# Four units of a banded attention transposed by VectorE and DMAs, with their products four steps later

## What is computed

```python
scores = jnp.einsum('bnqgrd,bnkgd->bngrqk', qb, kb) * (HEAD_DIM ** -0.5)
bias = -slopes[:, :, None, None] * dist[None, None]
scores = jnp.where(mask[None, :, None, None], scores + bias[None, None], -jnp.inf)
m = jnp.maximum(jnp.max(scores, axis=-1, keepdims=True), sink_l)
p = jnp.exp(scores - m)
denom = jnp.sum(p, axis=-1, keepdims=True) + jnp.exp(sink_l - m)
probs = (p / denom).astype(v.dtype)
out = jnp.einsum('bngrqk,bnkgd->bnqgrd', probs, vb)
```

## Time and profile before

| | us |
|---|---|
| median of 3 runs | 612.68 |
| lowest, highest | 609.06, 613.05 |
| the profiled execution | 608.62 |
| its span | 606.8 |
| granted clock of TensorE over the span | 0.999 of full |
| busy PE, DVE, ACT, POOL | 596.5, 447.3, 356.3, 293.6 |

### The profile page before, as it was taken

The page is one execution under the profiler, slowest core; times in us unless marked ns, Lnnn a source line. Parts: engine busy times, 40 slices in busy tenths (PEclk is TensorE's granted clock), DMA queues, the critical chain, the costliest instruction groups (busy, mean ns, idle before and its releaser), DMA issues.

```text
span 606.8 us, 9197 instructions
## 1 busy us (share of the span) xinstructions
PE 596.5 (98%) x3076; PEld 482.6 (80%) x3076; DVE 447.3 (74%) x802; ACT 356.3 (59%) x762; POOL 293.6 (48%) x273
## 2 busy tenths in 40 slices
PE   8999999999999999999999999999999999999996
PEld 7888887888888888888887777777767777888885
DVE  5786653334434439889999788998988988799884
ACT  6645133113333238777886678888788788534563
POOL 4610704415756432536547545876776776510601
PEclk9999999999999999999999999999999999999999
DMA  7598458574776620101005967868767745598042
GB/s 252 188 285 237 118 163 267 198 274 138 249 271 224 209 69 1 36 1 36 2 26 129 256 146 177 204 165 194 186 155 198 196 136 182 179 383 323 1 171 108
DMA packets 72431, 102.11 MB, mean 168 GB/s; under 512 B 10232, under 2 KB 43008, under 8 KB 72384
## 3 DMA queue, kind: packets, MB, share of 16 engines
q1 hardware_dynamic: 72224, 101.25, 55.6%
q10 hardware_dynamic: 160, 0.27, 0.1%
HBM read 60.17 MB, written 31.62 MB: 151 GB/s over the span
## 4 chain that ended last, share of the span: by engine, by line
PE 88%; DVE 4%; ACT 3%; DMA 2%; issue 1%; POOL 1%; SPq 0%; ACTq 0%
PE ps L1821 18%; PE ps L1823 17%; PE ps L1822 17%; PE ps L2115 8%; PE ps L2093 7%; PE ps L2023 5%; PE ps L2028 4%; PE ps L1993 3%; PE ps L2043 2%; PE ps L2003 2%; PE ps L1980 2%; PE ps L1979 2%; PE ps L2004 2%; ACT p_b L1221 1%; DVE pT_lo L1671 1%; DVE stat L1646 1%
## 5 line engine op out<-in xcount | busy, mean ns | idle before, releaser
L1671 DVE TENSOR_TENSOR pT_lo<-ps,pT_hi 128x512 fp32r<-128x512 f32 x102 | 68.8, 687 | 23.5 <-ACT pT_hi L1234 23.3
L1821 PE MATMUL ps<-hT_hi,w_hi 128*128 128x512 f32 x208 | 84.0, 404 | 0.0
L1221 ACT ACTIVATE p_b<-ps,stat 128x1024 f32<-128x1024 f32 x64 | 71.4, 1116 | 19.3 <-DVE stat L1646 19.0
L1823 PE MATMUL ps<-hT_hi,w_lo 128*128 128x512 f32 x208 | 81.4, 391 | 0.0
L1822 PE MATMUL ps<-hT_lo,w_hi 128*128 128x512 f32 x208 | 81.1, 390 | 0.0
L1646 DVE TENSOR_REDUCE stat<-ps 128x1 f32<-128x1024 f32 x64 | 76.6, 1215 | 2.1 <-PE ps L2043 2.0
L1234 ACT ACTIVATE pT_hi<-ps 128x512 fp32r<-128x512 f32 x102 | 59.9, 597 | 18.8 <-PE ps L2093 18.4
L2093 PEld LDWEIGHTS ps<-ident,p_b 128*128 128x128 f32 x408 | 47.9, 140 | 19.8 <-DVE pT_lo L1671 5.5
L2093 PE MATMUL ps<-ident,p_b 128*128 128x128 f32 x408 | 62.6, 276 | 0.5
L809 POOL TENSOR_SCALAR p_w<-p_w,stat 128x384 f32<-128x384 f32 (+1 forms) x40 | 24.4, 624 | 55.6 <-DVE stat L1554 55.6
L925 POOL TENSOR_TENSOR pT_lo<-p_land,pT_hi 128x512 fp32r<-128x512 f32 x26 | 33.0, 1291 | 30.5 <-ACT pT_hi L1241 30.5
(11 more groups left out here) (222 smaller groups left out, 1507.2 us busy)
## 6 DMA issues: line engine op xcount, KB each, us to landing
w_raw<-w_in SPq DMA_DIRECT2D x13, 512.0 KB, 4.4
probs_scratch<-p_blk SPq DMA_DIRECT2D x52, 128.0 KB, 2.8
p_land<-probs_scratch SPq DMA_DIRECT2D x13, 512.0 KB, 4.8
x_in<-x SPq DMA_DIRECT2D x8, 512.0 KB, 3.9
wt_raw<-w_out SPq DMA_DIRECT2D x8, 512.0 KB, 4.3
t_scratch<-wt_hi SPq DMA_DIRECT2D x16, 256.0 KB, 2.6
t_scratch<-wt_lo SPq DMA_DIRECT2D x16, 256.0 KB, 2.8
q<-q_h SPq DMA_DIRECT2D x16, 256.0 KB, 3.6
```

The source lines that it names most:

```text
L1221: nc.scalar.activation(p_b[:, (U + 1) % 4, :], ps[:, b:b + 2, :].rearrange("p b c -> p (b c)"), ACT.Exp, bias=nm_b[:, U % 4:U % 4 + 1], ac ...
L1671: nc.vector.tensor_tensor(pT_lo[at_], ps[:, 4 + a, :].rearrange("p (k c) -> p k c", c=P), f(pT_hi[at_]), ALU.subtract).then_inc(s_bTl, 1)
L1821: nc.tensor.matmul(o, a_hi, b_hi, start=first, stop=False, skip_group_check=goes_on)
L1823: return nc.tensor.matmul(o, a_lo, b_hi, start=False, stop=last, skip_group_check=goes_on)
```

## The change

Units 5, 7, 9 and 11 (`W_ROUTED`), all of g = 1, are no longer transposed by PE. For such a unit u:

- POOL scales all four heads (`POOL_HEADS` 4).
- DVE transposes 32x32 blocks of the whole unit, 1536 columns (`turn_w_probs`), in step u + 1 between the second and third maximum. SP stores with four DMAs and fetches with one (`store_w_probs`, `fetch_w_probs`). Unit 5's pair stands ahead of the wait for `s_wr` at `NM - 1`, those of 7, 9 and 11 behind it and behind the loads of `k_raw`.
- In step u + 3 ACT makes the high part of the whole unit (`routed_w_hi`, after the second exponential of steps 8, 10 and 12, after the fourth of step 14), and POOL the low part in two instructions (`routed_w_lo`), ahead of its scaling of unit u + 3.
- In step u + 4 PE makes its three pairs of products, behind the first two chunks' transposes of unit u + 3 and ahead of all gated work and of the products of unit u + 3. The outputs follow this new order (`W_ORDER`, `W_POS`).

Steps 6, 8, 10 and 12 have no transposes and no products left, steps 9, 11, 13 and 15 hold the products of two units. `beside` gives odd steps from 5 to 12 three thirds of a half job instead of four, and even ones five. The splits of blocks 11 and 12 move to steps 9 and 13. In step 16 the transposes of unit 15 come before any gated work. The diff, cut to its core:

```diff
+W_ROUTED = [5, 7, 9, 11]
+WR = len(W_ROUTED)
+POOL_HEADS = [3, 2, 2] + [2 if u in ACT_UNITS else 4 if u in W_ROUTED else 3 for u in range(3, 16)]
...
+            cut = 3 if 5 <= s <= 12 else 4
+            return N_WIN_JOB + (s + 1) // 2, range(cut) if s % 2 else range(cut, KT)
...
+        def w_now(s):
+            return [u for u in (s - 4, s - 1) if 0 <= u < W_UNITS and (u in W_ROUTED) == (u == s - 4)]
...
+            def store_w_probs(u):
+                i = W_ROUTED.index(u)
+                sp.wait_ge(s_pblk, NT + i + 1)
+                for q in range(4):
+                    sp.dma_start(pw_scr[i % 2, :, :, q, :].rearrange("a p c -> p a c"),
+                                 w_blk[q * Q32:(q + 1) * Q32]).then_inc(s_psto, 16)
+            def fetch_w_probs(u):
+                i = W_ROUTED.index(u)
+                sp.wait_ge(s_psto, 64 * (NT + i + 1))
+                if i >= 1:
+                    sp.wait_ge(s_wpv, W_FIRST[u - 2] + 3)
+                sp.dma_start(w_land, pw_scr[i % 2].rearrange("a p q c -> (a p) q c")).then_inc(s_pin, 16)
+            store_w_probs(5)
+            fetch_w_probs(5)
             sp.wait_ge(s_wr, NM - 1)
...
             load_k(0)
+            for u in (7, 9):
+                store_w_probs(u)
+                fetch_w_probs(u)
+            store_w_probs(11)
+            fetch_w_probs(11)
             sp.wait_ge(s_wr, NM)
...
+            def routed_w_lo(u):
+                pool.wait_ge(s_phi, NT + W_ROUTED.index(u) + 1)
+                for q in (slice(0, 2), slice(2, 4)):
+                    nc.gpsimd.tensor_tensor(w_low[:, q], w_land[:, q], f(w_high[:, q]), ALU.subtract).then_inc(s_plo, 1)
...
+                if s - 3 in W_ROUTED:
+                    routed_w_lo(s - 3)
                 if s < W_UNITS:
                     probs_w(s)
-                if s in (3, 7, 11):
-                    split_w(NM - 3 + (s - 3) // 4)
+                if s in (3, 9, 13):
+                    split_w(NM - 3 + (3, 9, 13).index(s))
...
+            def routed_w_hi(u):
+                i = W_ROUTED.index(u)
+                act.wait_ge(s_pin, 16 * (NT // 2 + i + 1))
+                act.wait_ge(s_ws, REP * 8)
+                if i >= 1:
+                    act.wait_ge(s_wpv, W_FIRST[u - 2] + 3)
+                nc.scalar.activation(w_high, w_land, ACT.Copy).then_inc(s_phi, 1)
...
+            def turn_w_probs(u):
+                i = W_ROUTED.index(u)
+                dve.wait_ge(s_wp, sum(POOL_HEADS[:u + 1]))
+                dve.wait_ge(s_ws, REP * 6)
+                if i >= 1:
+                    dve.wait_ge(s_psto, 64 * (NT + i))
+                nc.vector.transpose(w_blk.rearrange("p a (k c) -> p a k c", c=Q32),
+                                    p_w[:, u % 2, :, :].rearrange("p r (i a c) -> p a (r i) c", a=4, c=Q32)) \
+                    .then_inc(s_pblk, 1)
...
-                if s == W_UNITS:
-                    gated(g, ks[:len(ks) // 2])
-                    ks = ks[len(ks) // 2:]
                 for i in range(min(n, 2)):
-                    turn_w(s - 1, i)
+                    turn_w(u, i)
+                for v in now[:-1]:
+                    for i in range(3):
+                        pv_w(v, i)
+                    gated(g, ks)
+                    ks = ks[:0]
```

163 lines of the change are left out of this document (101 added, 62 removed).

## The result

| | before | after |
|---|---|---|
| median | 612.87 us of 4 runs | 645.24 us of 4 runs |
| lowest, highest | 609.06, 613.41 | 644.28, 648.36 |
| profiled execution, its span | 608.62, 606.8 | 644.88, 642.9 |
| granted clock over the span | 0.999 | 0.974 |

The change makes the kernel slower: ratio 1.0577, interval 1.0545 to 1.061. The two medians of the table alone would give 1.0528; the ratio isn't theirs, so the slowdown is known to about half a per cent. 642 was predicted, within 620 to 654. The span of the profiled executions grew by 36.1 us, and the banded stage by most of it.

What follows compares the result with a forecast made beforehand. PE and the softmax chain were taken as both the bound; 0.5 + 13.2 (three step pairs) + 10.7 (store) + 7.0 (end) = +31.4 us gave 640 from the profiled run, 644 from the median, said as 642, range 620 to 654.

Steps and rivals of the forecast that it cites:

- both: Main rival: both the costs of the step pairs and the store's stall occur, 640 to 644 us; chance 0.58.
- PE and the chain are both the bound: Banded stage: a unit's softmax, scores to scaling, takes 8.15 us and PE comes for its result 0.2 us later.
- Steps 6 and 7: First light and heavy steps: PE waits in the light step, spending the saved transposes' time; +0.5 us in all (0 to 1).
- The low half comes first: Steps 8, 10, 12: POOL's low half ahead of scaling delays the new unit's transposes from S+8.34 to S+10.2, +1.9 us each.
- The heavy odd step: Odd step behind steps 8, 10, 12 carries two units; hand-overs through bank 7 take T+8.2 instead of 5.7, +2.5 us.
- The store of unit 7: SyncE: the store waits for block 11's split, so ACT stands for the fetch and unit 10's transposes are late; +10.7 us once.
- The end of the stage: Steps 14 to 16: late transposes +4.3, step 15's second unit +1.3, step 16's order +1.4; together +7.0 us.
- The lock: POOL's low halves hold up DVE's small additions, up to 0.6 us in four steps, 2.4 us, only in the range.
- Only one of the two costs: Rival: the store comes in time or light steps hide more than walked; 620 to 634 us, chance 0.2.
- Faster: Rival: the transposes are pure PE time, 6.6 us saved; 602 us against the profiled run, 606 against the median, chance 0.04.
- worse: Rival: locks and slow reads come on top, 39 us and more; 650 to 660 us, chance 0.09.
- evened out: Rival: neither stall comes, the light steps cost PE what it saved; 606 to 618 us, chance 0.09.

Runs made afterwards that it cites:

- e5: Kernel before, with 32 products (7.4 us of PE's work) left out of gate jobs 19 to 22, output incomplete; 608.1 us, ratio 0.9974.
- e1: Changed kernel with all routed units' stores and fetches issued on SyncE ahead of the wait for block 11's split; 637.3 us, ratio 1.0439.
- e3: e1 with only unit 5 routed (W_ROUTED = [5]); 622.1 us, ratio 1.0193.
- e6: e1 with transposes of the identity added on PE in the waits of steps 7, 9, 11, 13 and 15; 632.0 us, ratio 1.0361.
- e7: e1 with routed products five steps later, high half at the end of ACT's step, low half behind the scaling; 637.2 us, ratio 1.045.
- e9: e1 with POOL's low half behind its scaling, and PE's gated work ahead of the old unit's products; 635.1 us, ratio 1.0412.
- e10: e7 with POOL's gate ahead of the low half; 639.6 us, ratio 1.0475.
- e14: e13 with unit 11 left to PE, splits of blocks 11, 12 and k_c in steps 7, 12, 8, step 16 as before; 624.0 us, ratio 1.0232.
- e2: Changed kernel with POOL's splits put back into steps 3, 7 and 11, SyncE's order unchanged; 636.1 us, ratio 1.043.
- e13: e10 with both halves one step later, in odd steps, and PE's gated work ahead of the routed products; 643.0 us, ratio 1.0534.
- e4: Kernel before with only the shares of three and five thirds of gated work and the later splits, no unit routed; 613.8 us, ratio 1.0058.

## Why the prediction was right

The way and the range were right; 645.24 us is 1.2 above the band of the main rival, *both*, 640 to 644. The stalls that were named are there and their sizes near, but the sum falls 4.7 us short of the 36.1 us of the profiled spans, and by the medians, 32.4 us, it is closer than its terms deserve. The range's upper end isn't what its words add up to: full locks and half of the slow reads, 2.4 and 2.8 us on 644, give 649 and not 654. Nothing hung on it.

**The bound.** The step "PE and the chain are both the bound" holds, and e5 shows that it was still too kind to PE: with 7.4 us less of PE's work the stage gains 0.8 us. The prediction's chain ends with the scaling; behind it a second one, the chunks' hand-overs, holds the other 5.76 us of a pair. The price of the removed transposes didn't matter.

**Steps 6 and 7**, 0.5: measured 0.7, and that it fits is luck. PE did wait (1.86 us ahead of T6), but in e1, e3, e6, e7, e9, e10 and e14, where the clock didn't fall in step 7, this pair takes 14.07 to 14.09 us, as long as before (14.05). In the changed kernel and in e2 and e13, where it fell, it takes 14.7 to 14.9. So the 0.7 us are the clock's, and the light step with its heavy neighbour cost nothing as long as no routed unit's products stood in it. Also, e4 shows a part I had no term for: the shares alone cost 0.66 us a pair. In step 6 of the changed kernel that is absorbed, since it has no transposes; in e3 it is paid where no unit is routed.

**The low half comes first**, +1.9: measured 2.0, and e9 takes it away by its cause. Low half S+8.8 expected, S+8.5 measured; its rate, the transpose's 1.77 us (1.85 put) and the high half's 1.47 us (1.6 put) were scaled up from rows of 1024 columns.

**The heavy odd step**, +2.5: mis-sized. It was 3.3 in step 9 and 3.5 in step 11, at a clock that had fallen, and 8.58 us, thus +2.8, in step 13 at the full clock. The e6 run has 8.6 us in all three. So the walk of hand-overs was short by 0.3 and the clock brought the rest.

**The store of unit 7**, +10.7: measured 11.5, by T10 at R+24.05 and not R+22.8. The mechanism is shown by e1 and e2 from two sides. The size was off in two places: the store to the fetch took 5.4 us, not 4.6, and k_raw with its second issue 1.4, not 0.8. The 4.6 us were read from stores of 128 KB, and these have 192. Before e1 I took the stall as worth all of its 12 us when removed. It was not: e1 gained 8.4 us by the ratio. Its place gave back 11.1, but the heavy steps took 2.7 of them, where the clock's fall now lay.

**The end of the stage**, +7.0: measured 7.2. S14 to T14 was 11.45 us, where I had S+11.8. The two small terms, 1.3 for step 15 and 1.4 for step 16, are not shown apart: in e4 and e14, where step 16 is as before, the span behind S15 is 1.7 us longer than before as well, and I have no cause for that.

**What wasn't in the sum**: 1.2 us ahead of S6, which the change doesn't explain. They lie ahead of the stage's first step: at 98 us PE waits 2.02 us where it waited 0.73, since a load of `lat` landed later. It is 0.8 us in e6 and 4.1 in e1, where the clock also fell around 100 us. The other part is the clock in the stage: 0.7 us in step 7, 0.4 and 0.7 in the two heavy steps that were longer than 8.6, and what it added to the stall and the end, which no run tells apart; between e1 and e6 it was some 4 us. The lock and the strips were in the range only. The strips cost nothing that can be seen: at the full clock the products from them start 0.24 us apart as others do (306.81 to 308.01 in e14, six of them). The lock lengthened additions by over 1 us, but beside POOL's work for which the chain waited anyway (0.33 us in step 8).

**The rivals.** "Only one of the two costs" fails, as both were there in full. "Faster" fails by e5, "worse" as the time is below its 650 and the reads cost nothing that shows. e14, with three units and the queues in better order, comes to 624: the rival "evened out" (606 to 618) would have needed the hand-over of bank 7 to be hidden as well. What remains open: whether a second output bank would bring the stage back to 56.15 us; all eight banks are in use in this stage, and it wasn't tried. By e5 it could hardly be faster than before. No kernel here that does all of the work came out faster than the one before.

## What to carry to other kernels

An engine at 98% is not yet worth relieving: compare the length of a step with the chains in it, here from its first product to the transposes that wait for the scaled result, and from these through ACT and DVE to the last product, and if they fill the step, take work off the engine in an experiment before moving it anywhere. A routed unit is free where its halves stand behind everything the current unit needs on ACT and POOL, its transfers ahead of any wait on SyncE, and its products where no other unit wants the same PSUM bank; each of these places cost 2 to 11 us when it was missed. And what stands last in the detour (a strip that a later load overwrites, as v_raw) gets later with it.

## What was unexpected in the hardware

- The granted clock of TensorE fell to 0.50 within the stage behind waits of PE of 1.86 and 3.81 us and in one of 6.95, and stayed at 1.00 after one wait of 3.84 us in the same kernel (and in e1 after one of 1.85). Transposes of the identity in the waits kept it at 1.00 (e6), which was worth some 4 us in 632.
- At the low clock, products of 512 columns started 0.43 us apart, at the high one 0.24.
- DVE additions of 128x4, 0.15 us by themselves, took 1.29, 1.49 and up to 1.79 us beside POOL's subtractions of 1.8 us each.
